# A two-block layer on one Trainium2 core: the second block's projection and mixer front end joined into one stage, and its first expert begun on all tokens

## The reference, cut to what matters

```python
def second_block(x, ...):
    h = h + _hybrid_mixer(_rmsnorm(h, norm_mix_w), ...)
    h = h + _expert_choice_ffn(_rmsnorm(h, norm_ffn_w), ...)
    return _rmsnorm(h, norm_final_w)

def _hybrid_mixer(xn, w_in, conv_w, ...):
    qkv, z, ab, u = split(xn @ w_in)               # 1536, 512, 16 and 512 columns
    q, k, v = split(silu(depthwise_conv5(qkv)))    # 4 heads of 128
    q, k = l2norm(q) * 128 ** -0.5, l2norm(k)
    # gated delta rule in chunks of 64, forward and backward: a triangular
    # system per head, chunk and side is solved, then a scan over 4 chunks
    o_delta = rmsnorm(o_fwd + o_bwd) * silu(z)
    o_pool = (centred_mean_pools_of(u, (2, 4, 8, 16)) - u) @ pool_w * pool_scale
    return concat(o_delta, o_pool) @ w_out

def _expert_choice_ffn(xn, router_w, w_gate, w_up, w_down):
    probs = softmax(xn @ router_w)                 # 16 experts
    gate, idx = top_k(probs.T, 32)                 # each expert takes 32 tokens
    h = silu(xn[idx] @ w_gate) * (xn[idx] @ w_up)  # 1024 -> 2048, per expert
    y = (h @ w_down) * gate                        # 2048 -> 1024
    return zeros.at[idx].add(y)
```

## Time and profile before

| | us |
|---|---|
| median of 3 runs | 2114.65 (2114.51 to 2116.11) |
| profiled execution | 2118.86 |
| its span | 2117.0 |
| granted TensorE clock, mean | 0.859 |
| TensorE / VectorE / ScalarE / GpSimd busy | 77% / 35% / 21% / 15% |
| DMA | 737.54 MB, mean 348 GB/s |

### The profile page before, as it was taken

One profiled execution on the slowest core, in us unless ns is written; L12 is line 12 of the kernel. 1 busy time (PEld: TensorE's weight loads), 2 busy tenths in 40 slices (PEclk: granted clock), 3 DMA queues, 4 the chain that ended last, 5 costly groups with the idle time before them and its releaser, 6 DMA issues. The chain is left out here.

```text
span 2117.0 us, 23616 instructions
## 1 busy us (share of the span) xinstructions
PE 1626.3 (77%) x9071; PEld 779.3 (37%) x9071; DVE 738.2 (35%) x1697; ACT 449.9 (21%) x992; POOL 315.6 (15%) x312
## 2 busy tenths in 40 slices
PE   7998879979777877789889766666666666766665
PEld 7987855545333333339678311111111110111110
DVE  4265267776777767654653200000000000000001
ACT  4255134222222312224531300000000000000001
POOL 0141033433433333310040000000000000000000
PEclk9998989989999999999989886778777777787777
DMA  7541389999999999986204899999999999999997
GB/s 267 170 128 61 130 327 379 419 420 421 419 421 421 420 420 421 421 340 239 110 14 174 357 420 420 419 420 420 421 421 420 420 421 421 421 420 420 421 420 313
DMA packets 111668, 737.54 MB, mean 348 GB/s; under 512 B 14048, under 2 KB 15968, under 8 KB 27616
## 3 DMA queue, kind: packets, MB, share of 16 engines
q1 hardware_dynamic: 74432, 467.86, 54.7%
q0 software_dynamic: 36864, 268.45, 30.6%
q10 hardware_dynamic: 288, 0.08, 0.0%
HBM read 735.30 MB, written 1.05 MB: 348 GB/s over the span
## 5 line engine op out<-in xcount | busy, mean ns | idle before, releaser
L2501 PE MATMUL ps<-arena,xe 128*32 128x512 f32 x2032 | 376.7, 832 | 194.2 <-DMA arena<-in_experts_in 194.2
L1123 PE MATMUL ps<-arena 128*128 128x512 f32 x820 | 404.1, 643 | 114.7 <-ACT arena L1302 114.6
L2658 DVE TENSOR_TENSOR low<-low,ps 128x512 f32<-128x512 f32 x16 | 11.0, 688 | 873.2 <-PE ps L2501 873.2
L1508 DVE CUSTOM_DVE_ANT_0 arena<-arena,ps 128x1024 f32<-128x1024 f32 x205 | 247.7, 1218 | 126.4 <-DMA arena<-in_peer,arena 126.3
L1123 PEld LDWEIGHTS ps<-arena 128*128 128x128 f32 x820 | 163.4, 205 | 336.4 <-issue 192.0
L1023 POOL DMA_INDIRECT arena<-in_peer,arena x205 | 196.2, 957 | 435.1 <-PE ps L1123 334.8
L2501 PEld LDWEIGHTS ps<-arena,xe 128*32 128x32 f32 x2032 | 47.3, 124 | 509.8 <-DMA arena<-in_experts_in 487.9
L2525 PE MATMUL ps<-arena,hT 128*32 128x512 f32 x1024 | 163.9, 743 | 78.6 <-DMA arena<-in_experts_down 67.4
L2690 POOL TENSOR_TENSOR low<-h,hT 128x512 f32<-128x512 f32 x2 | 2.5, 1270 | 933.8 <-DVE h L2671 933.8
L1302 ACT ACTIVATE arena<-ident,arena 128x128 f32<-128x128 f32 x256 | 83.7, 391 | 149.5 <-DVE arena L1518 145.2
L2525 PEld LDWEIGHTS ps<-arena,hT 128*32 128x32 f32 x1024 | 26.1, 122 | 198.9 <-DMA arena<-in_experts_down 160.7
(11 more groups left out here) (459 smaller groups left out, 1937.8 us busy)
## 6 DMA issues: line engine op xcount, KB each, us to landing
arena<-in_experts_in SPq DMA_DIRECT2D x254, 1024.0 KB, 26.9
arena<-in_experts_down SPq DMA_DIRECT2D x128, 1024.0 KB, 27.2
ring<-in_stream SPq DMA_DIRECT2D x42, 512.0 KB, 5.4
arena<-in_stream SPq DMA_DIRECT2D x36, 512.0 KB, 3.8
arena<-in_stream SPq DMA_DIRECT2D x14, 1024.0 KB, 7.1
arena<-in_peer,arena POOLq DMA_INDIRECT x205, 18.4
h<-in_x SPq DMA_DIRECT2D x1, 1024.0 KB, 5.0
arena<-in_sel SPq DMA_DIRECT2D x1, 1024.0 KB, 5.7
```

What stands on the lines that cost most here:

```text
L1123: last = nc.tensor.matmul(ps[:, 4 + 2 * t + half, :], diag[:, n % DIAGS, :], slot(n)[:, D + half * BANK:D + (half + 1) * BANK], start=firs ...
L1508: nc.vector.tensor_tensor_reduce(slot(n)[:, 0:D], slot(n)[:, 0:D], xrow(j // (QUADS // NT)), 1.0, 0.0, ALU.mult, ALU.add, act_in[:, u % 2, ...
L2501: last = nc.tensor.matmul(ps[32 * j:32 * (j + 1), 4 + r // KB, :], xe[:, k, :], w[:, j * BANK:(j + 1) * BANK], start=(k == 0), stop=(k == ...
```

## The change: what it does

- The projection has 20 units; units 2 to 19 are split in halves of 512 elements, the low halves on GpSimd instead of VectorE. The key columns come first, then queries, values, z and pools.
- The front end's work is done inside this loop, on each engine between its shares of the units. On TensorE, in the order shown below: `token_groups` 8 matmuls of 256 columns, `turn_groups` 2 transposes, `decay_rows` 5 narrow matmuls and 2 of 512 columns, `end_rows` (twice) 2 of 512 columns over 64 rows each, `beta_rows` 2 of 512, `sums` (twice) and `spread` (twice) 4 of 256 each, `key_products` 16 of 64 rows' output, `turn_keys` and `turn_values` 8 transposes each. The l2 norms are kept in four rows (`head_cols`, `head_rows`) in place of the diagonals. Taps read PSUM directly; sigmoid is computed by exp, so ScalarE's functions come in the order exp, ln, silu, exp, sqrt, silu, exp, sqrt, silu.
- The constants are one transfer of 1.9 MB into the first block's ring buffer, put in the queue between stream pieces 2 and 3.
- The Blocks of `second_block` and of the first part of `delta` are gone. During the inversion SyncE loads 4 + 2 expert pieces (the 2 into two new buffers, "seats"), and VectorE forms `qdec`, which GpSimd did before it. During the scan GpSimd forms the mean pools from running sums, TensorE multiplies them with `pool_w` in step 2.
- 20 pieces need no used piece; piece 20 + p needs piece p used, for p up to 11; from piece 32 on as before.
- Expert 0: its gate weights are stored by columns, 8 pieces of 256 columns. Gate pieces 0 and 1 are multiplied with all 256 tokens right after the router (`for_all_tokens`), and the 32 tokens are picked from the result by `open_chosen`. Up pieces come next (`open_up`), then gate pieces 2 to 7 (`open_gate`), each with 8 matmuls of 256 columns into one column group. The gather takes plain h in float32 with a one-hot scaled by the norm, expert 0's 32 columns first (16 matmuls of 32 columns, into `x0_ps`), the other 480 between the pieces; splitting and scaling h is gone.

```diff
+    ring2, F_UNITS = T.ring2, 20
+    M = T.mix = mixer_tiles(T)
...
+            for u in range(2, F_UNITS):
+                for hk in range(2):
+                    pool.wait_ge(f_high, 2 * u + hk + 1)
+                    high, low = half_parts(u, hk)
+                    nc.gpsimd.tensor_tensor(low, half_raw(u, hk), high.bitcast(F32), ALU.subtract).then_inc(f_low, 1)
...
-                if half == 0 and n >= 4:
-                    pe.wait_ge(f_kept, n - 3)
+                if half == 0 and 4 <= n < 10:
+                    pe.wait_ge(conv_done, n - 3)
...
-                            last.then_inc(ring2.used, 1)
-                last.then_inc(f_done, 1)
+                for hk in range(2):
+                    if u < 2:
+                        pe.wait_ge(first_lows, 2 * u + hk + 1)
+                    else:
+                        pe.wait_ge(f_low, 2 * (u - 2) + hk + 1)
+                    for m, (w, x) in enumerate(((wh, 0), (wl, 0), (wh, 1))):
+                        if u == 0 and m == 2:
+                            pe.wait_ge(fin_low, NT + hk + 1)
+                        for k in range(4 * hk, 4 * hk + 4):
+                            last = nc.tensor.matmul(ps[:, n % 4, half * S:(half + 1) * S], w[:, k, :], T.parts[:, x, k, :],
+                                                    start=(k == 0 and m == 0), stop=(k == KB - 1 and m == 2))
+                            if half == 1 and hk == 1 and m == 0 and k == 4:
+                                last.then_inc(ring2.used, 1)
+                    last.then_inc(f_half, 1)
+
...
             pe.wait_ge(fin_high, 2 * NT)
             for u in range(F_UNITS):
                 mix2_unit(u)
+                if u == 0:
+                    token_groups()
+                if u == 1:
+                    turn_groups()
+                if u == 5:
+                    decay_rows()
+                if u == 6:
+                    end_rows(0)
+                if u == 8:
+                    beta_rows()
+                    sums(0)
+                if u == 9:
+                    spread(0)
+                if u == 10:
+                    end_rows(1)
+                if u == 12:
+                    sums(1)
+                if u == 13:
+                    spread(1)
+                if u == 14:
+                    key_products()
+                if u == 15:
+                    turn_keys()
+                if u == 16:
+                    turn_values()
...
                 ring2.arrived(act, u // 2)
-                if u >= 2:
-                    act.wait_ge(f_done, u - 1)
-                nc.scalar.activation(parts_of(u)[0], raw2(u), ACT.Copy).then_inc(f_high, 1)
+                for hk in range(2):
+                    if u >= 2:
...
+            for u in range(F_UNITS):
+                if 2 <= u + 1 < F_UNITS:
+                    mix2_high(u + 1)
+                if u == 1:
+                    act.wait_ge(token_ps, 1)
+                    nc.scalar.activation(M.abT[0:16, :], ps[0:16, 6, 0:S], ACT.Copy).then_inc(ab_sb, 1)
+                if u == 2:
+                    centre_tap(0)
+                    softplus(link)
+                if u in (4, 6, 8, 10, 12):
+                    centre_tap(u // 2 - 1)
+                if u == 6:
+                    silu(0, M.qkT[:, 1, :, :])
+                if u == 8:
+                    decays()
+                    chunk_ends(0)
+                if u == 9:
+                    norm_root(0)
+                if u == 10:
+                    silu(1, M.qkT[:, 0, :, :])
+                if u == 11:
+                    chunk_ends(1)
+                if u == 13:
+                    norm_root(1)
+                if u == 14:
+                    silu(2, M.vT)
+                    keep_gate(6)
+                if u == 16:
+                    keep_gate(7)
+                if u == 17:
+                    keep_keys()
+                if u == 18:
+                    keep_pooled(8)
+            keep_pooled(9)
...
-            def mix2_low(u):
-                dve.wait_ge(f_high, u + 1)
-                high, low = parts_of(u)
-                nc.vector.tensor_tensor(low, raw2(u), high.bitcast(F32), ALU.subtract).then_inc(f_low, 1)
...
+            def taps(n):
+                dve.wait_ge(centre, 2 * n + 2)
+                for tap in (0, 1, 3, 4):
...
+                        y = M.part(b)[:, lo:hi]
+                        last = nc.vector.scalar_tensor_tensor(y, ps[:, n % 4, i * S + lo + off:i * S + hi + off], T.conv_w[:, b, tap:tap + 1], y,
+                                                              ALU.mult, ALU.add)
...
-                mix2_low(u)
+            first_low(1)
+            token_decay()
+            taps(0)
+            token_sources()
+            taps(1)
+            row_sums()
+            squares_of(0)
+            taps(2)
+            decay_products()
+            invert_root(0)
+            taps(3)
+            normalise(0)
+            squares_of(1)
+            taps(4)
+            invert_root(1)
+            taps(5)
+            normalise(1)
+            products_by_pairs()
+            dve.wait_ge(pairs_ps, 3)
+            nc.vector.tensor_copy(M.tok_v.rearrange("p t h d -> p (t h d)"), by_bank(6))
     stack.close()
...
+        @block.sync
+        def _(sync):
+            for i in range(FIRST_LOADS):
+                sync.dma_start(T.expert_ring.piece(i, 0), A["experts_in"][0, 0, i]).then_inc(T.expert_ring.sem_of(i, 0), 16)
+            for i in range(SEATS):
+                r = RING3 - 2 - SEATS + i
+                sync.dma_start(T.seats[i], A["experts_in"][0, 1, r - KB]).then_inc(T.seats_loaded[i], 16)
+
...
+                if n in (4, 6, 8, 10):
+                    g = n // 2 - 2
+                    rows = eg[:, :, g % 2, g // 2, :].rearrange("p c (h s) -> p h c s", h=DHEADS)
+                    cols = slice((g // 2) * P, (g // 2 + 1) * P)
+                    nc.vector.tensor_tensor(grp(qdec, g).rearrange("p h (c s) -> p h c s", c=2),
...
+                if st == 2:
+                    pe.wait_ge(pooled, 4)
+                    for i in range(4):
+                        last = nc.tensor.matmul(ps[:, i // 2, (i % 2) * S:(i % 2 + 1) * S], M.pool_w[:, i, :], window[i], start=True, stop=True)
...
-            for i in range(RING2, RING3 - 1):
+            for i in (8, 9, 10, 11, RING3, RING3 + 1, RING3 - 2):
                 first_lap(i)
             for i in range(FIRST_LOADS, RING2):
                 sync.wait_ge(ring2.used, G2_EXP - RING2 + i + 1)
                 first_lap(i)
-            for i in range(RING3, RING3 + 2):
+            for i in range(RING3 + 2, RING3 + 4):
                 first_lap(i)
-            sync.wait_ge(logits, 1)
-            first_lap(RING3 - 1)
 
             def load(q, pair):
                 r = q % PER
                 e = pair * 2 + q // PER
                 src = A["experts_in"][e, r // KB, r % KB] if r < 2 * KB else A["experts_down"][e, r - 2 * KB]
                 sync.dma_start(ring.piece(q, pair), src).then_inc(ring.sem_of(q, pair), 16)
-            for q in range(RING3 + 2, PAIR):
+            for q in range(RING3 + 4, PAIR):
                 sync.wait_ge(ring.used, ring.before(q) + 1)
+                if q == RING3 + 3 + DENSE:
+                    first_lap(RING3 - 1)
                 load(q, 0)
...
+            def for_all_tokens(c, t):
+                if t == 0:
+                    ring.arrived(pe, c)
+                w = ring.piece(c, 0).rearrange("p (k c) -> p k c", k=KB)
+                for k in range(KB):
+                    last = nc.tensor.matmul(ps[:, 2 + c, t * S:(t + 1) * S], hT[:, k, t * P:(t + 1) * P], w[:, k, :],
+                                            start=(k == 0), stop=(k == KB - 1))
+                if t == NT - 1:
+                    last.then_inc(ring.used, 1)
+
+            for_all_tokens(0, 0)
             pe.wait_ge(ex_p, 1)
             for t in range(NT):
                 last = nc.tensor.transpose(ps[0:NEXP, 5, t * P:(t + 1) * P], probs[:, t, :], ident[:, :])
             last.then_inc(pt_ps, 1)
+            for_all_tokens(0, 1)
+            for t in range(NT):
+                for_all_tokens(1, t)
             pe.wait_ge(rep_ready, 1)
...
 
+            pe.wait_ge(oh_first, NT)
+            for k in range(KB):
+                for t in range(NT):
+                    last = nc.tensor.matmul(ps[:, 0, k * CAP:(k + 1) * CAP], h[:, t, k * P:(k + 1) * P], onehot[:, t, 0:CAP],
...
             def gather(k):
-                if k >= 4:
+                if k == 0:
+                    pe.wait_ge(oh_ready, NT)
+                elif k >= 4:
                     pe.wait_ge(xg_sb, k - 3)
+                elif k == 2:
+                    pe.wait_ge(dense_sb, NT)
                 for t in range(NT):
-                    for a in range(2):
-                        last = nc.tensor.matmul(ps[:, k % 4, :], xs_parts[:, a, t, k * P:(k + 1) * P], onehot[:, t, :],
```

(54 more changed lines are left out.)

753 lines of the change are left out of this document (365 added, 388 removed).

## The result

The changed kernel takes 2120.57 us (median of 9 runs, 2116.59 to 2125.28), the kernel before 2116.11 us (9 runs, 2114.51 to 2118.73). The ratio is 1.0022, 95% interval 1.0012 to 1.0032: slower by 4.5 us. The forecast was 2113.0, 1.6 us faster; the time lies in the range 2100 to 2121, but the sign is the other one.

A forecast was written before the change was run, and what follows sets the result against it. The prediction took DMA as the bound from piece 32 on, and TensorE in the new opening. Experts stage 14.3 us earlier, piece 32 12.7 us later within it: -1.6 off the median 2114.65, 2113.0 us; 8-in-10 range 2100 to 2121.

The forecast's parts named there:

- What bounds the kernel: Experts stage: DMA is full, so the end is piece 32's landing plus a stream of 352 pieces that engines cannot shorten.
- A, the joined stage: Projection and front end as one loop: the inversion begins 16.8 us earlier, with 2.2 us of stalls counted.
- Rival 2: Joined loop: ScalarE's table loads and exponentials set the pace, up to 9.3 us more, 2115 to 2122; chance 0.20.
- rival 3: Joined loop: a ScalarE table switch costs 2.6 us where work is in flight, 5.3 us later, 2118; chance 0.04.
- B, inversion: Inversion: two more loads cost nothing under idle DMA, and `qdec` on VectorE is absorbed; no added time.
- B, scan: Scan: four `pool_w` products add 2.0 us and VectorE copies standing behind GpSimd's sums 0.5, together 2.5 us.
- C, the opening: Expert 0's opening: TensorE's chain to the 17th used piece makes piece 32 land 12.7 us later in the stage.
- rival 1: Opening: TensorE does not bind it, as column pieces cost what row-block pieces do; 17.7 us gained, 2097; chance 0.12.
- its hole: Sign in the opening: DMA idle for 15 to 20 us near 1200 to 1220, then no hole.
- the sentence on the clock: Opening: TensorE is never idle over 0.6 us, and where so busy its granted clock is 1.00 (2.4 GHz).
- Its spread "+-2": The opening's share, +-2 us, of the forecast's own range of 2107 to 2119.

The follow-up runs named there:

- `no_seats`: The changed kernel without the two expert pieces loaded into seats in the inversion (18 pieces preloaded): 2121.85 us.
- the opening alone: The kernel before with only the new opening of expert 0, its projection, front end, inversion and scan kept: 2132.80 us, ratio 1.0075.
- `waits_filled`: The changed kernel with its first gather moved into the wait for xe and its last into the wait for silu and the product with up: 2116.76 us.
- `halves`: The changed kernel with gate pieces by threes, gathers for other experts behind the gate, and expert 0's own tokens evicted in two halves: 2098.87 us.

## Why the forecast was wrong

*What bounds the kernel*: right. No stage of the stream moved, and the end is the time of piece 32 plus a constant: in the six profiles in which DMA is idle just ahead of piece 32 the span ends 895.7 to 896.7 us after the issue of piece 32.

*A, the joined stage*: right. From the first load to the inversion it is 17.0 us shorter (104.0 against 120.96; in all eleven profiles with the new stage 103.3 to 104.1), forecast 16.8. Rival 2, ScalarE's list as the pace, would have cost up to 9.3 us and has fallen: in the loop TensorE waited for the splits and for ScalarE only twice, 0.64 and 0.59 us, where the forecast had 2.2. So has rival 3: a load of a table in the joined loop takes 1.28 us between two operations, with 0.02 us before and nothing after it. The Trainium skill, "ScalarE: Activation LUTs", section "What ACT_TABLE_LOAD costs", adds a drain of about 1.38 us; these rows show none.

```profile
993.33 0.82 ACT L1448 ACTIVATE arena<-ps,conv_w 128x256 f32<-128x256 f32 x2
994.17 1.28 ACT L1467 ACT_TABLE_LOAD   x1
995.46 1.15 ACT L1467 ACTIVATE arena<-arena 128x512 f32<-128x512 f32 x2
```

*B, inversion*: wrong. "Two more loads ... lie under these 35.6 us, in which DMA is idle: nothing", and `qdec` "absorbed". The inversion grew by 1.9 us in the mean of the three profiles of the table (36.95 against 35.03). In all seven profiles with six pieces loaded there TensorE stands still for 1.3 to 1.7 us some 15 us after the first load, with nothing released ("issue"); with four pieces for 0 to 0.6 (four profiles), with the inversion of before, whose four pieces are issued 15 us ahead of it, 0.3 at most (three). Lengths: 37.2 us in the mean of the seven, 36.1 of the four, 35.3 of the three. So 1.1 us go with the two loads, and 0.8 with what else is new there, `qdec` among it, which was not tried alone. DMA's packets by queue in the changed kernel from 1045 to 1064 us (packets, MB, share):

```profile
q1 hardware_dynamic: 864, 6.29, 82.3%
q8 instruction: 3, 0.05, 1.1%
```

Three packets of code stand beside 864 of weights. The second of them starts 11.8 to 12.2 us after the inversion's first product in all seven profiles with six pieces and 10.7 to 10.9 in the four with four. It starts ahead of TensorE's stop, so its lateness is no effect of the stop. That fits code held up by the weights; whose code it is the trace does not say, and the cause is not proven.

Without the two loads the kernel was no faster all the same. In all four profiles with four pieces the scan that follows took 45.1 to 45.4 us at a granted clock of 0.92, in the seven with six pieces 42.2 or 43.8 at 1.00 or 0.96. Inversion and scan together took 80.1 us in the mean with six pieces and 81.4 with four. Why the clock differs is not shown.

*B, scan*: nearly right. Forecast +2.5; it took 2.9 more at the same granted clock of 0.96 (43.8 against 40.9), and 2.9 more in the mean of the three. At 1.00 it takes 42.2, at 0.92 45.4: the same 384 instructions. These are the changed kernel again, and `no_seats`:

```profile
1082.90:1126.70 43.80, 42.03 (x384) 36.09 (x384) 21.23 (x42) 9.31 (x23) 11.15 (x15) 0.96 0.01 1
```

```profile
1080.70:1126.10 45.40, 43.60 (x384) 37.43 (x384) 21.23 (x42) 9.30 (x23) 11.21 (x15) 0.92 0.00 1
```

*C, the opening*: the mechanism was right, the size was not. TensorE binds it, the gate pieces are the dearest term (rival 1 has fallen), and DMA has its hole. Forecast +12.7 us; the profiles say +14.5 (first against first) and +16.0 (means), the opening alone +16.1 by the medians and +17.3 in its profile. The step that failed is the sentence on the clock: "where it is busy so the granted clock is 1.00". Its own rows spoke against it: in the scan of the earlier trace rows TensorE is 96% busy and the granted clock is 0.96. In the opening the clock fell in two places: two up pieces took 3.57 us at 1170.97 and 1.92 at 1176.28; six down pieces 7.05 against 5.36. Of the second fall only 0.8 us come before the 17th piece is used, so up to there the two cost 2.5 us. The chain came out 1.6 longer than forecast (95.5 against 93.9); in the two further profiles it was 97.0 and 97.2, with a third fall in both (the first eight products of `for_all_tokens` took 5.39 us instead of 3.70). That is 2.7 us of the 3.3 in the mean. The other 0.6 is the reference: the first profile of before, from which the forecast took its 1226.15, was longer there than the mean of the two (959.57 against 958.99).

The rest of the chain met its forecast partly by luck. The eight gathers took 1.81 us each between two begins, not 1.63: 1.4 more. `open_chosen`, priced at 1.7, ran beside the first gate piece and cost nothing. From the router to `x0` it was 15.2 us, priced at 16.0.

*The sum*: -17.0 + 1.9 + 2.9 + 16.0 = +3.8 instead of -16.8 + 0 + 2.5 + 12.7 = -1.6. None of the four terms is far out, and three are out to the slower side: the opening by 3.3 us, the inversion by 1.9, the scan by 0.4. This is what a difference of two terms of 15 us does: each has to be right within a tenth for the sign to be.

*The range and the rivals.* No rival that ends on the slower side named the opening. Its spread "+-2" about a term priced wholly at full clock should have been lopsided: the clock can only cost there. Two microseconds for the clock, the size of one fall at either end of the chain, would have moved the forecast to no change.

## What to carry to other kernels

Before work is moved onto an engine that has reserve, count what of the reserve the new chain eats: here TensorE had 15 us in the opening and was given 29 (from the router to the 17th piece 69.3 us instead of 40.1), so the change turned a stretch bound by DMA into one bound by TensorE, and sensitive to its clock. Products of 32 columns of weights all in one column group leave the other groups unused; three pieces in three groups took here the time of one. Price a chain on TensorE with a fall of its clock or two, about 1.7 us each here. And work that the first piece of a stream does not need (gathers for later experts) belongs behind it, where the engine waits for DMA anyway.

## What the runs showed of the hardware

- Three gate pieces, 24 products of 256 columns in three column groups in turn, took 3.6 us, as one piece of 8 products in one group (3.64). Even `open_chosen` (group 0) and the first gate piece (group 1) ran side by side without being asked to: both begin at 1187.27 and 1187.28, and that piece too was done in 3.6 us.
- TensorE stood still for 1.3 to 1.7 us in the inversion in all seven profiles in which six pieces of 1 MB were queued at its begin, and for 0.6 at most in the four with four; where they were left out, the scan behind it ran at a lower granted clock (0.92) in all four.
- The scan, whose 384 instructions follow each other closely, comes in lengths of 42.2, 43.8 and 45.1 to 45.4 us, at a granted clock of 1.00, 0.96 and 0.92: about 1.6 us for each step.
- In all eight profiles with the joined stage and the new opening the clock fell 46 to 47 us into the experts stage, at the first up pieces or at the gather put ahead of them (`waits_filled`), and also where TensorE had not waited (`halves`). In the four of them with a granted clock under 1.00 in the scan it was low at the begin of `for_all_tokens` as well (5.39 us instead of 3.70); in the four with 1.00 it was not.
